# Retrieving PEER experts for 256 of 576 tokens: a dense up product beside choice and gates, then rows of V fetched by index

## The reference: one layer with a PEER block

```python
q = (xb @ w_pq).reshape(blk, 8, 2, 128)
s = einsum('nhpd,hpkd->nhpk', q, peer_keys)              # scores against 128 keys per half
s_top, i_top = top_k(s, 16)
cand = s_top[:, :, 0, :, None] + s_top[:, :, 1, None, :]  # 16 x 16 sums per head
g_s, g_i = top_k(cand, 16)
e = take_along_axis(cand_idx, g_i)                        # expert = i * 128 + j
g = softmax(g_s)                                          # the gates
act = gelu(einsum('nd,nhkd->nhk', xb, peer_u[e]))
out = einsum('nhk,nhkd->nd', g * act, peer_v[e])          # 128 rows of V per token
```

## Time and profile before

| | us |
|---|---|
| median of three runs | 3191.28 |
| span of the profiled execution | 3195.1 |
| TensorE busy (share of the span) | 2866.6 (90%) |
| VectorE busy | 1910.5 (60%) |
| ScalarE busy | 1048.6 (33%) |
| GpSimd busy | 384.6 (12%) |

### The profile page before, as it was taken

How to read it: one execution, slowest core, us unless ns; L and a number is a source line. 1 busy time by engine, 2 the same in 40 slices (tenths; PEclk the granted TensorE clock), 3 DMA queues, 4 the chain that set the end, 5 groups by cost and what they waited for, 6 DMA issues and landing times. The chain is left out here.

```text
span 3195.1 us, 47076 instructions
## 1 busy us (share of the span) xinstructions
PE 2866.6 (90%) x15273; PEld 2291.1 (72%) x15273; DVE 1910.5 (60%) x3793; ACT 1048.6 (33%) x1485; POOL 384.6 (12%) x487
## 2 busy tenths in 40 slices
PE   7979988876898795378999999999999999999997
PEld 3434535555744495357999999999888888888886
DVE  1348736463012368897998888887555555555554
ACT  1112330011202221354445555554333333333332
POOL 0010134101000131360002122221000000000000
PEclk9976795556797697689999999999999999999998
DMA  3000023213220120125666566666555445554543
GB/s 151 10 15 1 15 82 107 76 53 105 107 118 7 42 64 17 69 121 207 209 217 211 203 236 211 238 214 211 189 173 172 163 167 169 170 173 163 175 169 117
DMA packets 206678, 424.82 MB, mean 133 GB/s; under 512 B 20449, under 2 KB 129378, under 8 KB 203618
## 3 DMA queue, kind: packets, MB, share of 16 engines
q1 hardware_dynamic: 191170, 371.23, 34.4%
q0 software_dynamic: 10784, 47.99, 3.9%
q10 hardware_dynamic: 4608, 4.20, 0.4%
HBM read 381.61 MB, written 41.74 MB: 132 GB/s over the span
## 5 line engine op out<-in xcount | busy, mean ns | idle before, releaser
L1929 PE MATMUL psC<-xh,Uh 128*128 128x256 f32 (+1 forms) x2048 | 608.2, 297 | 0.0
L1929 PE MATMUL psC<-xl,Uh 128*128 128x256 f32 (+1 forms) x2048 | 604.3, 295 | 0.0
L1929 PE MATMUL psC<-xh,Ul 128*128 128x256 f32 (+1 forms) x2048 | 603.4, 295 | 0.0
L1948 PE MATMUL psC<-Vh,Wh 128*128 128x512 f32 x1280 | 502.9, 393 | 14.4 <-DVE Wl L1870 9.7
L1948 PE MATMUL psC<-Vl,Wh 128*128 128x512 f32 (+1 forms) x1280 | 502.6, 393 | 0.0
L1827 DVE TENSOR_TENSOR Vl<-rV,Vh 128x1024 fp32r<-128x1024 f32 x256 | 320.1, 1250 | 232.3 <-ACT Vh L1770 232.3
L1770 ACT ACTIVATE Vh<-rV 128x1024 fp32r<-128x1024 f32 x256 | 271.4, 1060 | 413.7 <-PE psC L1948 413.3
L1948 PE MATMUL psC<-Vh,Wl 128*128 128x512 f32 x1024 | 402.2, 393 | 0.0
L1929 PEld LDWEIGHTS psC<-xh,Uh 128*128 128x128 f32 x2048 | 385.4, 188 | 15.1
L1929 PEld LDWEIGHTS psC<-xh,Ul 128*128 128x128 f32 x2048 | 385.4, 188 | 8.8
L1929 PEld LDWEIGHTS psC<-xl,Uh 128*128 128x128 f32 x2048 | 385.3, 188 | 0.0
(11 more groups left out here) (279 smaller groups left out, 3739.5 us busy)
## 6 DMA issues: line engine op xcount, KB each, us to landing
rU<-in_peer_uT SPq DMA_DIRECT2D x256, 512.0 KB, 4.4
rV<-in_peer_v SPq DMA_DIRECT2D x256, 512.0 KB, 3.5
gates<-gst POOLq DMA_DIRECT2D x18, 2048.0 KB, 7.4
gr<-gates SPq DMA_DIRECT2D x32, 640.0 KB, 6.0
arena<-in_poolM SPq DMA_DIRECT2D x128, 128.0 KB, 2.1
gr<-gates SPq DMA_DIRECT2D x32, 512.0 KB, 5.5
wraw<-in_w_pq SPq DMA_DIRECT2D x16, 512.0 KB, 3.3
arena<-in_w_in SPq DMA_DIRECT2D x8, 884.0 KB, 15.9
```

The lines of the kernel that those rows point to most:

```text
L1929: last = M(bank(6 + k, hi - lo), a[:, k, c], x[:, d, lo:hi], start=(d == 0 and a is Uh and x is xh), stop=(d == KD - 1 and x is xl))
L1948: last = M(bank(2 * b + n, p1=m), w[:, k, b * P:b * P + m], v[:, k, c], start=(first and a == 0), stop=(final and a == len(parts) - 1), sk ...
```

## The change

The blocks get two roles: DENSE = 0, 1 and 4 (320 tokens) and GATHER = 2 and 3 (256 tokens). `peer_dense` becomes two blocks.

`peer_up` runs the up product alone, for the 256 tokens of GATHER: 128 steps of 24 matmuls of 256 columns, with no gelu, no V and no down. ScalarE copies the raw result to hst and GpSimd stores it, four steps at a time, in a new DRAM tensor `hidden`. All five choices and the 80 units of the dense 320 tokens stand beside these steps (a part per step for 24 steps, then 9 parts in 25 steps and 4 units in 5). A unit changes: ohI as before, but VectorE now compares and weighs in one instruction per token (`tensor_scalar`, four of 128 columns), so ohJ and GpSimd's multiply go. For the two GATHER blocks VectorE makes lists of indices (rowV, eltH).

`peer_down` is dense PEER for the 320 tokens, the same matmuls as the second group before: 24 of 320 columns and 16 of 512 in a step. The high part Wh is copied by ScalarE now. Beside it GpSimd issues 512 indirect DMAs: 256 of one 4-byte element per partition (from `hidden`) and 256 of one 4 KB row of V per partition (512 KB each), into eight slots. VectorE adds each row, times its gate and activation, to h or to a second sum, odd: 256 instructions over 1024 columns, 64 of them per 25 steps from step 24 on.

```diff
 peer_select
-            for t in range(2):
-                for part in range(CHOICE_PARTS):
-                    choice_part(V, dve, C, t, part, *best_of(t), [w[:] for w in wide])
...
+def peer_up(nc, T, sems, C, xh, xl, IT, JT, cT, G, hidden):
...
+    FIRST = 2 * CHOICE_PARTS
+
+    def parts_before(s):
+        return min(PARTS, s if s < FIRST else FIRST + (s - FIRST) * 9 // 25)
+
+    def units_before(s):
+        return min(NU, max(0, s - FIRST) * 4 // 5)
...
         @block.vector
...
+            def one_hots(u):
...
+                V.tensor_tensor(ohI[:, u % 4, :, :], keys,
+                                IT[:, TU * u:TU * u + TU].unsqueeze(2).broadcast_to([P, TU, NKEY]), ALU.is_equal)
+                for a in range(TU):
+                    c = TU * u + a
+                    last = V.tensor_scalar(ohC[:, u % 4, a, :], iota, JT[:, c:c + 1], cT[:, c:c + 1],
+                                           ALU.is_equal, ALU.mult)
+                last.then_inc(S["oh_done"], 1)
...
+            for s in range(NKEY):
+                if s + 2 < NKEY:
+                    low_u(s + 2)
+                for o, part in parts_at(s):
+                    choice_part(V, dve, C, o, part, wide)
+                    if part == CHOICE_PARTS - 1 and o >= len(DENSE):
+                        indices(o)
+                for u in units_at(s):
+                    one_hots(u)
...
         @block.tensor
...
+            for s in range(NKEY):
+                up(s)
+                for o, part in (parts_at(s - 1) if s >= 1 else ()):
+                    if part == CHOICE_PARTS - 1 and o < len(DENSE):
+                        choice_turn(nc, pe, C, o, bank(0))
+                for u in (units_at(s - 1) if s >= 1 else ()):
+                    weights(u)
...
+def peer_down(nc, T, h, sems, xh, xl, G, hidden):
+
+
+    SLOTS = 8
+    NV = len(GATHER) * P
+    START = 24
+
+    def sums_before(s):
+        return min(NV, max(0, s - START) * 64 // 25)
...
         @block.gpsimd
...
+            def element(b, k):
+                pool.indirect_dma_start(G.hid[:, b, k:k + 1], None, elements,
+                                        bass.IndirectOffsetOnAxis(ap=G.eltH[:, b, k:k + 1], axis=0))\
+                    .then_inc(hid_in[b], 16)
+
+            def row(b, k):
+                m = b * P + k
+                if m >= SLOTS:
+                    pool.wait_ge(S["acc"], m - SLOTS + 1)
+                pool.indirect_dma_start(gbuf[:, m % SLOTS, :], None, experts,
+                                        bass.IndirectOffsetOnAxis(ap=G.rowV[:, b, k:k + 1], axis=0))\
+                    .then_inc(row_in[m % SLOTS], 16)
+
+            for k in range(P):
+                element(0, k)
+            for k in range(P):
+                row(0, k)
+                element(1, k)
+            for k in range(P):
+                row(1, k)
...
         @block.scalar
...
+                for b in range(len(GATHER)):
+                    if opens(s + 1, b):
+                        act.wait_ge(hid_in[b], 16 * P)
+                        A(G.hid[:, b, :], G.hid[:, b, :], ACT.Gelu).then_inc(S["hid_ge"], 1)
...
         @block.vector
...
+            def add_row(m):
...
+                dve.wait_ge(row_in[m % SLOTS], 16 * (m // SLOTS + 1))
+                if m >= 2:
+                    dve.wait_ge(S["acc"], m - 1)
...
+                    V.scalar_tensor_tensor(out=a, in0=x, scalar=w, in1=a, op0=ALU.mult, op1=ALU.add)\
+                        .then_inc(S["acc"], 1)
...
 build
...
+            peer_select(nc, T, h, ctx, C, *x, range(spent[0], spent[-1] + 1))
+            peer_up(nc, T, ctx, C, *x, *IJ, G, hidden)
+        peer_down(nc, T, h, ctx, *x, G, hidden)
```

More of the change, by code:

```diff
@@ L66, in toks, with cols, block_a @@
     return slice(t * P, t * P + rows(t))
-def block_a(nc, T, h, sems):
+DENSE = [0, 1, NBLK - 1]
+GATHER = [2, 3]
+ORDER = DENSE + GATHER
+ND = 2 * P + NS
+NG = 2 * P
+def cols(t):
+    at = sum(rows(x) for x in ORDER[:ORDER.index(t)])
+    return slice(at, at + rows(t))
+def block_a(nc, T, h, sems, kept):
     ctx = ExitStack()
@@ L1272, with choice_part @@
 CHOICE_PARTS = 12
-def choice_part(V, dve, C, t, part, mv, mi, wide):
+def choice_part(V, dve, C, o, part, wide):
+    t = ORDER[o]
     R, S = rows(t), C.sems
+    mv, mi = C.mv[:, t], C.mi[:, t]
     m4 = mv.rearrange("p (h a) k -> p h a k", a=2)[0:R]
@@ L1635, in peer_dense @@
+        hst = sb("hst", [P, 2, 4, NG])
         ohI = sb("ohI", [P, 4, TU, NKEY])
-        ohJ = sb("ohJ", [P, 4, TU, NKEY])
         ohC = sb("ohC", [P, 4, TU, NKEY])
         gst = sb("gst", [P, 2, NKEY, CH])
[L1639 to L1645, removed]
+        wide = [sb(f"wide{i}", [P, PH, PK, PK], BF16)[:] for i in range(3)]
@@ L1650, in peer_dense @@
+        h_out = [sems.enter_context(nc.semaphore(f"c_h_out{i}")) for i in range(2)]
         block = ctx.enter_context(nc.Block())
[L1652 to L1665, removed]
@@ L1755, in _ @@
+            for i in range(2):
+                pool.wait_ge(h_out[i], 16 * (QG // 2))
+                pool.wait_ge(g_out[i], 16 * (NCH // 2))
         @block.scalar
@@ L1912, in weights, with up @@
                 last.then_inc(S["oh_used"], 1)
-            for r in range(4):
-                weights(r, r)
-            with pe.Fori(1, UP // 4) as i:
-                for r in range(4):
-                    weights(4 * i + r, r)
-            def up(g, s, k):
-                lo, hi, _ = GROUPS[g]
+            def up(s):
+                pe.wait_ge(S["lU"], s + 1)
+                if s >= 4:
+                    pe.wait_ge(S["h_ev"], s - 3)
+                for d in range(KD):
+                    c = slice(d * P, (d + 1) * P)
+                    for a, x in ((Uh, xh), (Ul, xh), (Uh, xl)):
+                        last = M(bank(UPB[s % 4], NG), a[:, s % 3, c], x[:, d, ND:NTOK],
+                                 start=(d == 0 and a is Uh and x is xh), stop=(d == KD - 1 and x is xl))
+                last.then_inc(S["u_mm"], 1)
@@ L2028, in build @@
 def build(nc, T):
+    hidden = nc.dram_tensor("hidden", (P, NKEY, NG), F32, kind="Internal").ap()
     ctx = ExitStack()
```

589 lines of the change are left out of this document (313 added, 276 removed).

## The result

The changed kernel takes 2903.49 us (median of four runs, 2902.28 to 2907.16) against 3190.66 us for the kernel before beside it: a ratio of 0.9099, interval [0.908, 0.9117]. That is 9% faster, but 239 us more than the 2664 forecast and above the range of 2610 to 2800. The profiled execution has a span of 2901.8 us.

What follows compares the result with a forecast made beforehand. Both old groups were taken as TensorE-bound, with 195 us of little TensorE work. Terms 1259 + 77 + 338 + 14 + 928 + 35 + 17 gave 2668 us of span, 2664 us forecast, range 2610 to 2800.

Steps and rivals of the forecast that it cites:

- P up to 24 x 7.17 / 128 = 1.34 us is free: Down stage, GpSimd: an indirect DMA's queue cost, taken as 1.14 us, costs nothing up to 1.34 us.
- the prediction's own law: Down stage: 128 elements in by step 24, then rows and elements share 50 steps at 1.40 us each, later 2.8 a row.
- The term of 35 us: Down stage, steps 24 to 74: DMA transfers of 7.8 to 8.1 us exceed TensorE's 7.17, adding 35 us (bounds 0 and 100).
- the price of the elements: Down stage until step 74: 2.56 x 8 element packets per DMA engine, 1.0 us a step.
- the excess of 50 us: Down stage: at about 358 GB/s of HBM, rows fill the DMA engines in all 100 steps, some 50 us extra.
- the term 80 x 0.40: Up stage, other 104 steps: TensorE's 80 units at 0.40 us each, within 3.16 us a step, 328 us.
- the start at 1259 us: Start of the up stage: first load, split and block begin after the last key search put the first up at 1259 us.
- 77 us for the first steps: Up stage, first 24 steps: VectorE sets the pace at 3.23 us a step, 77 us.
- 928 us for the dense steps: Down stage: TensorE's matmuls are those of the old second group, so its 928 us stand.
- GpSimd holding VectorE: Rival, down stage: a DMA per row sum holds VectorE, 8.85 us a step, 168 us more, 2797 us; chance 0.08.
- The slower indirect DMA: Rival, down stage: an indirect DMA costs 1.4 to 2.0 us on GpSimd, 2752 us at 1.7, 2867 at 2.0; chance 0.17.
- row sums wait for rows: Sign in the down stage: if seen with DMA share well under 1.0, the indirect DMA's cost on GpSimd is the bound.

Runs made afterwards that it cites:

- wider: Changed kernel with the first 128 element fetches taking 128 bytes an index instead of 4, into their own tile; 2859.39 us.
- late run: Changed kernel with GpSimd's first element issued only after TensorE did 8 down-stage steps, row sums opening at step 32 instead of 24; 2811.08 us.
- float32r run: Changed kernel with the one-hot tiles of the 80 units in float32r, so a unit is 4 TensorE passes instead of 8; 2898.96 us.
- even run: Changed kernel with fetches handed out by TensorE step, elements of both blocks spread, activated in eighths, rows from step 12; 2676.29 us, ratio 0.8381.
- one by one: Changed kernel with each element fetch waiting for the one before it to land, row sums opening at step 40; 3053.08 us.
- spaced: Changed kernel with a 384-column GpSimd memset behind every element fetch, row sums from step 30; 2748.34 us.

## Why the prediction was wrong, and where it was right

**The step that failed** is the one on GpSimd: "P up to 24 x 7.17 / 128 = 1.34 us is free". With VectorE idle P was sized well (0.94 + 0.30 us against 1.14), and by the prediction's own law, elements in by step 24, it would have been free. Beside VectorE it was too small: 1.19 + 0.30 = 1.49 us in the 50 steps, above the 1.40 that the law allows there, and 1.80 + 0.30 in the steps after them, so row sums and splits do not leave P alone. But VectorE waits for no row in either, so this is not where the time went. What the law left out is that GpSimd without a pause costs TensorE. The runs show it: 167 us in the first steps and most of 72 us beside rows, both gone without elements, and gone with all of them at 1.64 us. Why the stall lasts is argued and not shown. The rows suggest that it feeds itself: beside a working VectorE the fetches come every 1.43 to 1.47 us (the wider and the late run), about slow enough; once TensorE stalls, VectorE stands still, they come every 1.25 us, and it lasts until GpSimd stops.

**The term of 35 us** for the DMA engines was the wrong mechanism. The 50 steps did lose 72 us, but at a DMA share of 0.84; at 0.98 without elements, and at 0.92 to 0.95 with them at a slower pace, nothing is lost. What was mis-sized is the price of the elements, 1.0 us a step. From 1758 to 1800 us of the changed kernel the 35 fetches that GpSimd issues are all that queue q0 moves (packets, MB, share of the 16 engines):

```profile
q0 software_dynamic: 1056, 0.02, 1.9%
```

That is 0.80 us of all engines, 0.023 us a fetch and 0.06 us for 2.56 of them, and 3.55 + 3.5 + 0.06 us stay within 7.17.

The Trainium skill, DMA: Bandwidth & Descriptors, section Specifications, has some 358 GB/s of HBM per core as a bound; the trace agrees that it can be reached (357 GB/s in the run without elements), and TensorE lost nothing there, so the excess of 50 us that the prediction worked out from it did not come either. The 414 GB/s of the earlier trace rows lie above it.

**The up stage**: the term 80 x 0.40 was half of what it is, by a row read as two units that was one. With 0.80 TensorE needs 2.85 + 0.62 = 3.47 us a step, 360 us, and the stage took 376; with the first 24 steps that is 451 us, above the 410 to 440 expected. The float32r run shows how near VectorE's bound lies: 14 of the 32 us come back.

**What held**: the start at 1259 us, 77 us for the first steps, 14 us between the blocks, row sums of 1.28 us beside the dense work without VectorE as bound, and 928 us for the dense steps: the even run's stretch of 957.6 us is the sum's 994 without its 35. Of the rivals, GpSimd holding VectorE did not happen (a row sum stays at 1.28 us). The slower indirect DMA did, beside VectorE, but not its price: the sign "row sums wait for rows" is absent in the changed kernel and seen only in the runs one by one and spaced. The nearness of 957.6 to 959 holds for a kernel that issues otherwise than the one predicted.

**What stays open** is what GpSimd's indirect DMAs share with TensorE's instructions. The Trainium skill, SBUF — State Buffer, section Who interferes with whom, says that TensorE waits on nobody and that DMAs have ports of their own; by that rule there would be no stall, and here the measurement decides. That a row fetch alone at 1.25 us does the same was not tried.

## What to carry to other kernels

An indirect DMA must be costed twice: for the time on GpSimd, and for its pace beside TensorE. Here one every 1.6 us, handed out step by step, was free, and one every 1.25 us without a pause took nearly all of TensorE; tie the issue to the progress of the matmuls instead of letting GpSimd run ahead. And count an instruction's records (640 for 80 units) before dividing a row's time by them.

## What was not expected of the hardware

Beside indirect DMAs issued every 1.25 us TensorE executed one instruction per 1.40 us with nothing to wait for, at a DMA share down to 0.01 and a granted clock of 0.50 (1.2 GHz), while plain loads every 0.60 us from the same engine left it alone. The time of a fetch hardly goes by its indices (0.83 us for 16, 0.94 for 128, VectorE idle in both) and much by what VectorE does beside it (1.80 us for a row beside row sums and splits).
